# Two gates computed inside their FFN stages, two halves of modulation moved out of the first block's passes, and the last expert's product by halves

## The reference, cut to what matters

```python
# first block, one layer
mod = silu(c) @ w_ada + b_ada          # 6 vectors of 1024: sh1, sc1, gt1, sh2, sc2, gt2
h = rmsnorm(x) * (1 + sc1) + sh1
x = x + gt1 * token_mixers(h, ...)     # window attention, gMLP, differential attention
x = x + gt2 * hier_moe(rmsnorm(x) * (1 + sc2) + sh2)   # 16 experts, 2 of one group per token
# second block, two layers
mod = silu(c_2) @ ada_w[l] + ada_b[l]  # 9 vectors: sh, sc, ga for each of three stages
x = x + 0.5 * ga1 * swiglu(norm(x) * (1 + sc1) + sh1)        # FFN, hidden width 2816
x = x + ga2 * token_mixing(norm(x) * (1 + sc2) + sh2)
x = x + 0.5 * ga3 * swiglu(norm(x) * (1 + sc3) + sh3)        # FFN
```

## Time and profile before

| what | value |
|---|---|
| median of 3 runs | 2058.75 us (2058.44 to 2060.17) |
| the profiled execution | 2059.59 us, its span 2057.8 us |
| PE, PE weight loads busy | 1944.5 us (94%), 1728.8 us (84%) |
| DVE, ACT, POOL busy | 1371.2 us (67%), 988.7 us (48%), 84.7 us (4%) |
| mean clock granted to PE over the span | 0.966 of full speed |
| HBM traffic | 455.43 MB read, 222 GB/s over the span |

### The profile page before, as it was taken

The page is one execution under the profiler, slowest core; times in us unless marked ns, Lnnn a source line. Parts: engine busy times, 40 slices in busy tenths (PEclk is TensorE's granted clock), DMA queues, the critical chain, the costliest instruction groups (busy, mean ns, idle before and its releaser), DMA issues.

```text
span 2057.8 us, 29861 instructions
## 1 busy us (share of the span) xinstructions
PE 1944.5 (94%) x12656; PEld 1728.8 (84%) x12656; DVE 1371.2 (67%) x1459; ACT 988.7 (48%) x1143; POOL 84.7 (4%) x107
## 2 busy tenths in 40 slices
PE   7998889999998999999999899999999999999998
PEld 3977778888886999999877799989998997778997
DVE  4888568988897777666435687768765453465444
ACT  3345357777775433354444443344334544445332
POOL 1330100000000100000000000000000000000000
PEclk9988979999999999999999999999999999999999
DMA  8565338989996587545322487757863542124554
GB/s 359 219 229 187 155 126 335 372 345 355 361 361 231 227 324 290 203 188 205 143 80 82 164 311 290 279 204 297 296 225 144 185 184 83 62 104 183 184 184 154
DMA packets 63877, 458.42 MB, mean 223 GB/s; under 512 B 7040, under 2 KB 7296, under 8 KB 8832
## 3 DMA queue, kind: packets, MB, share of 16 engines
q1 hardware_dynamic: 63744, 456.51, 59.1%
HBM read 455.43 MB, written 1.05 MB: 222 GB/s over the span
## 4 chain that ended last, share of the span: by engine, by line
issue 60%; PE 25%; DVE 7%; DMA 3%; ACT 2%; POOL 1%; DVEq 1%; POOLq 0%; ACTq 0%; SPq 0%
PE PS L356 7%; PE PS L358 7%; PE PS L357 7%; DMA ada<-in_ada 2%; DVE acc L329 2%; DVE wlo L283 2%; PE PS L932 1%; ACT whi L277 1%; PE PS L1199 1%; DMA raw<-in_stream 1%; DVE hlo L465 1%; POOL Z L488 1%; PE PS L904 0%; ACT Z L444 0%; PE PS L1263 0%
## 5 line engine op out<-in xcount | busy, mean ns | idle before, releaser
L283 DVE TENSOR_TENSOR wlo<-raw,whi 128x2048 fp32r<-128x2048 f32 x282 | 646.3, 2294 | 355.3 <-ACT whi L277 350.1
L277 ACT ACTIVATE whi<-raw 128x2048 fp32r<-128x2048 f32 x282 | 538.5, 1913 | 354.8 <-PE PS L358 316.3
L356 PE MATMUL PS<-whi,hhi 128*128 128x256 f32 (+1 forms) x1568 | 506.2, 323 | 26.9 <-DVE wlo L283 12.2
L358 PE MATMUL PS<-whi,hlo 128*128 128x256 f32 (+1 forms) x1568 | 494.4, 315 | 0.0
L357 PE MATMUL PS<-wlo,hhi 128*128 128x256 f32 (+1 forms) x1568 | 494.3, 315 | 0.0
L356 PEld LDWEIGHTS PS<-whi,hhi 128*128 128x128 f32 x1568 | 305.9, 195 | 50.1 <-issue 14.9
L356 PE MATMUL PS<-hhi,whi 128*128 128x256 f32 x1152 | 326.6, 284 | 2.2 <-DVE mod L351 2.2
L358 PE MATMUL PS<-hhi,wlo 128*128 128x256 f32 x1152 | 326.0, 283 | 0.0
L357 PE MATMUL PS<-hlo,whi 128*128 128x256 f32 x1152 | 326.0, 283 | 0.0
L358 PEld LDWEIGHTS PS<-whi,hlo 128*128 128x128 f32 x1568 | 305.3, 195 | 17.0
L357 PEld LDWEIGHTS PS<-wlo,hhi 128*128 128x128 f32 x1568 | 306.2, 195 | 15.6
(11 more groups left out here) (390 smaller groups left out, 1804.4 us busy)
## 6 DMA issues: line engine op xcount, KB each, us to landing
raw<-in_stream SPq DMA_DIRECT2D x285, 1024.0 KB, 4.9
ada<-in_ada SPq DMA_DIRECT2D x92, 1024.0 KB, 5.0
ada<-in_stream SPq DMA_DIRECT2D x48, 1024.0 KB, 4.9
raw<-in_ada SPq DMA_DIRECT2D x3, 1024.0 KB, 15.7
xs<-in_x SPq DMA_DIRECT2D x1, 1024.0 KB, 11.8
Z<-in_ada SPq DMA_DIRECT2D x1, 1024.0 KB, 19.6
Z<-in_ctx SPq DMA_DIRECT2D x1, 1024.0 KB, 11.3
masks<-in_masks SPq DMA_DIRECT2D x2, 512.0 KB, 9.6
```

Of the source, the lines that this page charges most:

```text
L277: nc.scalar.activation(whi[:, s], src, ACT.Copy).then_inc(hi_ready, 1)
L283: nc.vector.tensor_tensor(wlo[:, s], src, whi[:, s].bitcast(F32), ALU.subtract).then_inc(lo_ready, 1)
L356: nc.tensor.matmul(out_, ah, bh, start=start, stop=False, skip_group_check=check)
L358: return nc.tensor.matmul(out_, al, bh, start=False, stop=stop, skip_group_check=check)
```

## The change

`EARLY_HALVES` goes from 18 to 16, so the passes make halves 8 to 15 and no longer 16 and 17, and `ATT_STEPS` is written anew (64 steps instead of 80). All later halves move two places earlier; the FFN stage (1, 0), which made 8, makes 10. For the FFN stages of layer 0 the gate's vector is then not there when the stage begins, so its row is made inside: DVE scales the column in group 2, PE makes one half of the row behind the half sum of group 4 and the other behind that of group 5, and ACT copies each. Stages of layer 1 and the mixing stages keep their gates. In the first expert tile `route_act(1)` stands behind the first conversion, followed by a Silu of one column. The last expert's down product goes over the output halves first, and its split and scatter follow half by half.

```diff
-EARLY_HALVES = 18
-QKV_HALVES = (28, 29)
-FFN_HALVES = {(0, 0): (18, 10), (0, 1): (30, 10), (1, 0): (40, 8), (1, 1): (48, 0)}
+EARLY_HALVES = 16
+QKV_HALVES = (26, 27)
+FFN_HALVES = {(0, 0): (16, 10), (0, 1): (28, 10), (1, 0): (38, 10), (1, 1): (48, 0)}
+GATE_AT = (4, 5)
...
+        def gate_inside(k, l):
+            return l == 0 and k != 1
+        def gate_half_pe(pe, N, k, l, i, bank):
+            if i == 0:
+                pe.wait_ge(*N.diag.at(k, l))
+            for c in range(4):
+                ins = nc.tensor.matmul(PS[:, bank, c * P:(c + 1) * P], ones, diag[:, 4 * i + c], start=True, stop=True)
+            ins.then_inc(*(N.row_mm.up if i else gate_half_mm.up))
+        def gate_half_act(act, N, k, l, i, bank):
+            act.wait_ge(*(N.row_mm.at(k, l) if i else gate_half_mm.at(k // 2)))
+            nc.scalar.activation(row[:, 512 * i:512 * i + 512], PS[:, bank], ACT.Copy).then_inc(*(N.row.up if i else gate_half_row.up))
...  (hidden_pe)
-            gate_pe(pe, N2, k, l, 6)
+            inside = gate_inside(k, l)
+            if not inside:
+                gate_pe(pe, N2, k, l, 6)
             head_turn(pe, 0, h0)
...
-            pe.wait_ge(*N2.row.at(k, l))
+            if not inside:
+                pe.wait_ge(*N2.row.at(k, l))
...
+                if inside and g - 1 in GATE_AT:
+                    pe.wait_ge(*(N2.row.at(k, l) if g - 1 == GATE_AT[1] else gate_half_row.at(k // 2)))
                 gate_up(pe, g, 0, c0, E0)
...
                     half_sum(pe, v0 + g - 1, 2 * (1 - g % 2) + 1)
+                if inside and g in GATE_AT:
+                    gate_half_pe(pe, N2, k, l, GATE_AT.index(g), 2 * (1 - g % 2))
                 if g <= TAIL:
                     pe_down(pe, g - 1, c0, E0, h0)
...  (hidden_act: gate_half_act behind act_hi of groups 4 and 5; hidden_dve, group 2:)
+                if g == 2 and gate_inside(k, l):
+                    dve.drain()
+                    layer_gate(dve, k, l)
...
-        ATT_STEPS = [4, 5, 3, 5, 2, 3, 3, 0, 3, 3, 3, 2, 0, 3, 1, 3, 3, 3, 3, 2, 3, 2, 3, 3, 3, 3, 3, 1, 2, 2, 1, 0]
+        ATT_STEPS = [3, 4, 3, 4, 2, 2, 2, 0, 2, 3, 2, 2, 0, 2, 1, 2, 3, 2, 3, 2, 2, 2, 2, 3, 2, 3, 2, 1, 2, 1, 0, 0]
...  (moe_pe, the last tile)
-            moe_down_pe(pe, MOE_N - 1)
-            for t in range(NT):
-                moe_scatter_pe(pe, t, (MOE_TILES - 1,)).then_inc(y_sum, 1)
+            for half in range(2):
+                w = slice(half * 512, half * 512 + 512)
+                for c in range(4):
+                    wh, wl = us[c // 2]
+                    ins = mm3(PS[:, 4 + half], he_hi[:, c], he_lo[:, c], wh[:, c % 2, w], wl[:, c % 2, w], False, c == 3)
+                if half == 0:
+                    ins.then_inc(*last_half.up)
+            ins.then_inc(unit_used, 2)
+            for half in range(2):
+                w = slice(half * 512, half * 512 + 512)
+                pe.wait_ge(*part_lo.at(2 * b + half))
+                for t in range(NT):
...  (moe_act, first tile)
                 conv_hi(act, c + RING)
+                if n == 0:
+                    route_act(act, 1)
+                    nc.scalar.activation(sm[:, 255:256], k1[:, K1["eps"]][:, 0:1], ACT.Silu)
                 conv_hi(act, c + 1 + RING)
```

More of the change, by code:

```diff
@@ L89 @@
 PE_HALVES = 4
-EARLY_HALVES = 18
+EARLY_HALVES = 16
 SPLIT_HALVES = ()
-QKV_HALVES = (28, 29)
-FFN_HALVES = {(0, 0): (18, 10), (0, 1): (30, 10), (1, 0): (40, 8), (1, 1): (48, 0)}
-assert FFN_HALVES[0, 1][0] >= B1_HALVES + 18 and FFN_HALVES[1, 1][0] == N_HALVES
+QKV_HALVES = (26, 27)
+FFN_HALVES = {(0, 0): (16, 10), (0, 1): (28, 10), (1, 0): (38, 10), (1, 1): (48, 0)}
+GATE_AT = (4, 5)
+assert FFN_HALVES[0, 1][0] >= B1_HALVES + 16 and FFN_HALVES[1, 1][0] == N_HALVES
 def columns(fields):
@@ L673, in hidden_act @@
             conv_hi(act, c0 + 1 + RING, E0)
-            gate_act(act, N2, k, l, 6)
+            if not gate_inside(k, l):
+                gate_act(act, N2, k, l, 6)
             act_hi(act, 0, c0, E0, h0)
@@ L686, in hidden_act @@
                     act_hi(act, g, c0, E0, h0)
+                    if gate_inside(k, l) and g in GATE_AT:
+                        gate_half_act(act, N2, k, l, GATE_AT.index(g), 2 * (1 - g % 2))
                     conv_hi(act, c + 2 + RING, E0)
@@ L692, in hidden_act, with hidden_dve @@
                         conv_hi(act, c + 2 + RING, E0)
-        def hidden_dve(dve, c0, E0, h0, halves):
+        def hidden_dve(dve, c0, E0, h0, halves, k, l):
             v0, nh = halves
@@ L867, in bass_network @@
         xg_made = Signal(N1.fullB.sem, 1, 6)
+        gate_half_mm, gate_half_row = Signal(x_hi.sem, 1, 2 * MOE_TILES), Signal(x_lo.sem, 1, 2 * MOE_TILES)
+        last_half = Signal(x_mm.sem, 1, 2 * MOE_TILES)
         def slots(b):
@@ L984, in moe_pe @@
                 moe_scatter_pe(pe, t, range(MOE_TILES - 1))
-            moe_down_pe(pe, MOE_N - 1)
-            for t in range(NT):
-                moe_scatter_pe(pe, t, (MOE_TILES - 1,)).then_inc(y_sum, 1)
+            n, b = MOE_N - 1, MOE_TILES - 1
+            pe.wait_ge(hlo_done, n + 1)
+            us = [[w.rearrange("p (k n) -> p k n", k=2) for w in unit(pe, moe_down(n) + q)] for q in range(2)]
+            for half in range(2):
[10 more added lines that the diff above has]
+                for t in range(NT):
+                    out_ = PS[:, OUT_BANK[t][half]]
+                    nc.tensor.matmul(out_, picked[b][:, t * P:(t + 1) * P], part_hi[b][:, w], start=False, stop=False)
+                    ins = nc.tensor.matmul(out_, picked[b][:, t * P:(t + 1) * P], part_lo_[b][:, w], start=False, stop=True)
+                    if half:
+                        ins.then_inc(y_sum, 1)
         def moe_spread_act(act, b):
@@ L1013, in moe_part_act @@
         def moe_part_act(act, b):
-            act.wait_ge(unit_used, moe_down(MPG * b + MPG - 1) + 2)
             for half in range(2):
+                if b == MOE_TILES - 1 and half == 0:
+                    act.wait_ge(*last_half.at(0))
+                else:
+                    act.wait_ge(unit_used, moe_down(MPG * b + MPG - 1) + 2)
                 w = slice(half * 512, half * 512 + 512)
@@ L1430, in act_block1 @@
             moe_spread_act(act, 0)
-            route_act(act, 1)
             moe_act(act)
@@ L2161, in pool_layer, with layer_gate @@
                     nc.gpsimd.memset(fr, 1.0).then_inc(*B["zeroed"].up)
+        def layer_gate(dve, k, l):
+            gate_dve(dve, N2, mod2[:, 72 * l + 24 * k + 16:72 * l + 24 * k + 24], 1.0 if k == 1 else 0.5)
         def dve_prepare(dve, k, l):
@@ L2166, in dve_prepare @@
             factors_dve(dve, N2, mod2[:, 72 * l + 24 * k + 8:72 * l + 24 * k + 16], s2_all[:, l, S2["ng"]][:, 8 * k:8 * k + 8], am)
-            gate_dve(dve, N2, mod2[:, 72 * l + 24 * k + 16:72 * l + 24 * k + 24], 1.0 if k == 1 else 0.5)
+            if not gate_inside(k, l):
+                layer_gate(dve, k, l)
         def dve_layer(dve, l):
@@ L2178, in dve_layer @@
                 spread_dve(dve, N2, 0, 0, 1, hhi, hlo, shift2(0, 0), TB, am)
-            hidden_dve(dve, FF0, E0, l * (2 * FFN_GROUPS) + MOE_N, FFN_HALVES[l, 0])
+            hidden_dve(dve, FF0, E0, l * (2 * FFN_GROUPS) + MOE_N, FFN_HALVES[l, 0], 0, l)
             dve_prepare(dve, 1, l)
@@ L2434, in dve_layer @@
             norm_dve(dve, N2, 2, l, shift2(2, l), FF1, E0, (B["y_half"].at(0, l), (unit_used, E0 * 3 + (WO0 + 4))))
-            hidden_dve(dve, FF1, E0, l * (2 * FFN_GROUPS) + MOE_N + FFN_GROUPS, FFN_HALVES[l, 1])
+            hidden_dve(dve, FF1, E0, l * (2 * FFN_GROUPS) + MOE_N + FFN_GROUPS, FFN_HALVES[l, 1], 2, l)
             y_at = [(y_sum, l * 4 + 5 + t) for t in range(NT)]
```

## The result

| kernel | median, us | runs | ratio |
|---|---|---|---|
| before | 2059.34 | 2058.44 to 2060.17 | 1 |
| after | 2045.02 | 2044.41 to 2045.58 | 0.9929 [0.9917, 0.9942] |

The change makes the kernel 0.71% faster, 14.3 us. The prediction was wrong: it had said 2053.9, and the result lies 1.5 under 2046.5, the lower end of its range; the same kernel measured once more, 2046.41, lies 0.1 under it. The profiled execution took 2044.41 us with a span of 2042.6; the one of before 2059.59 and 2057.8, so the two spans differ by 15.2. In the new file the half steps are L324 and L330, the half sum L343, the maximum L1782, the exponential L1452, the turn in the passes L1338, `head_turn` L555, `dve_h` L617.

The account below looks back on a forecast made before the run. It took TensorE to bound FFN stages, and VectorE with its loads or TensorE the passes. -10.0 + 3.6 + 1.7 + 1.1 - 1.7 + 0.4 = -4.9 gave 2053.9 us, range 2046.5 to 2060.5.

Parts of the forecast that it names:

- The passes, -10.0: Attention passes: two halves fewer, sixteen VectorE steps of 764 ns less, save 10.0 us; bounds -2 and -15.
- a ring of load, steps and exponential: In the passes VectorE waits 8.2 us for `ada` loads, the exponential follows VectorE, and TensorE waits 9.2 us for it.
- By thirds: Passes' gain: 1.5 us up to pass 8, 5 from 8 to 20, 3.6 from 20 on, 0.5 in the tail.
- up to pass 8 four projections fill TensorE: First part of the passes: VectorE loses four steps, but only 1.5 us can go.
- The bound of -15: Passes' largest gain: TensorE's idle time, lost clock and half sums all go, except for the GELU.
- Rival 1: Passes freed altogether: ring breaks, clock stays up, -15 in place of -10, total -9.9, 2048.9 us; chance 0.12.
- The gates, +3.6: Stages (0, 0) and (0, 1): each 1.8 us longer, nothing won in the head; bounds +3.0 and +4.4.
- The clock behind the new waits, +1.7: Heads of (0, 0) and (0, 1): one of two new 2.15 us waits lowers TensorE's clock; bounds 0 and +3.4.
- Stage (1, 0), +1.1: FFN stage (1, 0) makes ten halves for eight and takes 1.1 us longer; bounds 0.6 and 2.9.
- The last expert, -1.7: End of the experts: by halves, the residual starts 1.7 us earlier; bounds -1.0 and -2.2.
- First expert tile, +0.4: First expert tile: the exponential comes later, first `wlo` 0.7 later, TensorE waits 0.4 us; bounds 0 and +1.3.
- What would show it: Signs expected in the profile after, for passes, waits, FFN heads, stages and the residual behind the experts.

Follow-up runs that it names:

- the repeated run: The changed kernel measured once more, unaltered: 2046.41 us, ratio 0.9928 to the kernel before.
- experiment 4: The kernel before, with the loads of halves 8 to 17 in the passes cut to 64 of 2048 columns: 2052.36 us, ratio 0.9958.
- experiments 3: The kernel before, with the half steps of halves 8 to 17 in the passes over 64 of 512 columns: 2040.92 us, ratio 0.9901.
- experiment 10: The changed kernel with the half steps of halves 8 to 15 in the passes over 64 of 512 columns: 2041.91 us, ratio 0.9908 to before.
- experiment 1: The changed kernel with halves 16 and 17 back in the passes, all else of the change kept: 2062.31 us, ratio 1.0009 to before.
- experiment 5: The changed kernel with `dve_h` ahead of the half steps in the FFN heads: 2050.92 us, ratio 0.9945 to before.
- experiment 7: The changed kernel with the last expert's down product and its scatter put back whole: 2053.05 us, ratio 0.9960 to before.
- experiment 6: The changed kernel with the second routing exponential back ahead of the first conversion, the Silu of one column dropped: 2047.73 us, ratio 0.9935 to before.
- experiment 11: The changed kernel with `dve_h` ahead of the half steps and the first half sum moved out of the FFN heads: 2041.09 us, ratio 0.9907 to before.

## Why the prediction was wrong, point by point

In short: the passes were forecast to give 10 us, 15 at the most, and gave 18.2 (17.2 in the repeated run). VectorE with its loads held TensorE back through most of them, and TensorE ran at its lower clock for a fifth of the time. I had priced only a part of either.

- **The passes, -10.0 with bounds -2 and -15: this is the step that failed. It measured -18.2, and -17.2 in the repeated run.** The mechanism was seen, a ring of load, steps and exponential, but priced as if it bound only in some passes. By thirds (1.5 + 5 + 3.6 and 0.5 forecast) the passes gave 4.1 up to pass 8, 1.15 of it by the clock of the first pass, 8.9 from 8 to 20, 5.2 from there. Three errors of sizing are in it. First, "up to pass 8 four projections fill TensorE": with VectorE out of the way that third takes 31.2 us even in before, against 34.6, so TensorE did not fill it. VectorE also loses five steps there and not four. Second, the loads: the waits of 8.2 us fell to 2.6, and experiment 4 prices them with their clock at 9.2; I had counted on most of one of them and left the others standing. Third, the clock: only the stretch behind pass 17 and a short one were to go. Before the change TensorE spent some 20 us of the passes at the lower level (four stretches, from 147, 160, 184 and 215 on) besides the first 3.5 us, after it none but the first microsecond. The third of them, in windows of the kernel before, with the 4 us ahead of it in which TensorE waits 2.59 us for VectorE and the exponential:

```profile
180.00:184.00 4.00, 1.68 (x10) 1.06 (x9) 1.68 (x3) 0.56 (x1) 0.00 (x0) 1.00 0.81 291
184.70:191.40 6.70, 6.70 (x28) 5.67 (x27) 5.01 (x11) 3.05 (x9) 0.00 (x0) 0.50 0.41 157
```

  Busy 6.70 of 6.70 looks like an engine at its limit, and is one at half its clock. The last third came out nearest: 28.7 us by the later of VectorE and TensorE for each pass, 27.2 measured (six passes from 20 on had three steps, not seven).
- How the 18.2 divide: 4.6 for two halves whose work on VectorE is small already (their two half sums are 1.6 by the prediction's price; the rest was not taken apart), 13.6 for VectorE's hold on the passes (experiments 3 and 10), about 0.8 of that by the first pass. How much of the rest is clock was not measured by itself, and one price does not fit all stretches: in the first pass an estimated 2.5 us more of the lower level (clocks of 0.89 over 4.32 us and 0.68 over 5.42) cost 1.10 us, behind the GELU 3.5 us of it cost nothing that shows (87.19 and 87.29). For the 20 us of before only bounds can be estimated: from nothing to half of them, 10 us.
- The bound of -15 was said to be TensorE's idle time, the lost clock and the half sums. Its own terms come to more: the waits of 9.2 without the 2.34 at the GELU are 6.9, the half sums 1.6, and a clock of 0.89 over 109.8 us is an estimated 24 us at the lower level, up to 12 us lost. Together that is up to 20.5, and -18.2 lies inside. So the term that was sized too small in the bound is the lost clock, or the idle time with it. Rival 1 named what happened, with 0.12 and a size of -15, and its objection, that two steps and a maximum take as long as TensorE's pass, was no reason: the passes did come down to within 4.2 of TensorE's pace.
- **The gates, +3.6:** right, +1.80 and +1.79. Nothing was won in the heads, since `dve_h` set the turn; the wait is 1.99 for the 2.15 forecast.
- **The clock behind the new waits, +1.7 with bounds 0 and +3.4:** it measured 0 in both heads, in both profiled executions of the changed kernel; the lower bound. That is in part luck: behind the same wait of 2.00 in the head of (0, 1) the clock did fall in experiment 1, and stage (0, 1) took 1.46 us more. In experiment 5 it fell behind waits of 1.63 at the half sums.
- **Stage (1, 0), +1.1:** 1.5, within its bounds.
- **The last expert, -1.7:** right, -1.57 in the profiled executions and 1.8 by experiment 7. The total of experiment 7 is 6.6 longer, the rest by the clock elsewhere.
- **First expert tile, +0.4:** the forecast wait is there, 1.0 and 0.5 us in the two executions; experiment 6 shows no cost of the move.
- The other terms together are +3.6 where +5.1 was forecast. The passes alone moved the time out of the range: with -18.2 in place of -10 the sum would have been 2045.7, against 2045.0.
- "What would show it" named 10 us less (18.2), waits under 4 (2.6) and about 4 (2.9), the idle time in the heads (there), the stages 2 us longer (1.8) and a residual about 2.0 us behind the end of the last down product (637.71 to 639.96, 2.25).

What stays open: why the kernel with seventeen halves lost in the mixing stage of layer 1 what it won, beyond that its clock is lower there; and how the 13.6 us divide between idle time and clock. The second would need a kernel in which TensorE's clock stays up while VectorE's steps are full, and no kernel here is one.

## What to carry to other kernels

Where an engine off the busiest one feeds it through a ring (load, elementwise work, exponential, product), do not take the busiest engine's measured busy time as the floor where its clock is lowered. TensorE was busy 100.80 of 109.80 us at a clock of 0.89, and with VectorE's steps short, in the same kernel, the passes took 92.10. Rather count the time at the lower level too, and let the upper bound of a gain reach to the engine's pace at the full clock. Before a difference of one profiled execution is put down to a change, profile the same program again: here the first pass differed by 1.1 us between two executions of one program. And when a wait is taken out of one place, look at the next instruction that needs the displaced work: the head's 2 us moved to the half sum with one edit and vanished only with two.

## What the runs showed that I had not expected

- Time given back to VectorE in the passes cost about 1.6 to 1.9 times its length (4.9 us of reductions: 8.4 and 9.4, or 8.0 and 8.3 without the first pass), whether in one piece or in four.
- A stretch of 3.5 us at the lower clock behind the GELU cost nothing in the passes, though TensorE was busy all through it: without the first pass the two executions took 87.19 with it and 87.29 without. Experiments 5, 6 and 7 have it too, with 87.29, 87.23 and 87.15, and experiment 11 has not, with 87.08.
- With the last expert's product whole, stretches of the lower clock lay elsewhere in a stage 500 us later, which was 5.9 us longer; whether the shift of 2 us did it or chance is not shown. Changes of a few microseconds in this kernel are better judged by the stage that they touch; the total carries a spread of about 5 us from run to run (2044.41 to 2049.48 for one program).
- A half step over 64 columns takes 295 ns and one over 512 takes 761 (the groups of VectorE in experiment 10 and after): 1.04 ns for each column and some 230 ns that do not depend on them. By this estimate, two steps of half the width would cost more than one.
